# Two products of the same weights by one matmul of 512 columns in four residual stages

## The chip, the cores and the metric

The kernel runs on one core of a Trainium2 chip. The metric is the device time of one execution in microseconds (us), taken as the median of several. A profiled execution gives a trace; its span is the time from its first to its last instruction.

## The reference

Two blocks work on x of 256 tokens by 1024 features. Each adds to x what gated branches bring. Only the shape of the places where x is changed matters here:

```python
# first block, layer 0: z = h @ w_in, a convolution branch y_a and a recurrent branch y_b
return jnp.concatenate([y_a, y_b], axis=-1) @ p["w_out"], hT
# first block, layer 1: pooled branch
return (y * jax.nn.silu(g)) @ p["w_out"]
# both layers
x = x + gate[:, None] * out_x
# second block: token mixers end in a product with w_o, then the feed-forward part
x = x + mod[:, 2, None] * mix_x
x = x + mod[:, 5, None] * swiglu(h2, w_up[l], w_down[l])
```

After each of these four additions comes a norm over the 1024 features of x (the root of the mean of squares), and the next stage starts from the normed x. All inputs are fp32.

## The kernel before

**Layout.** Everything is feature-major: x is [128, 8, 256], eight slices of 128 features with all 256 tokens (`T`) as columns. A product with weights is made one output tile of 128 features at a time. A weight tile is [128, 8, 128], 512 KB, and SP loads them from one stream into a ring of six buffers `raw` (L420); a load waits until the tile six places ahead of it has been used. `ORDER` fixes the order of all tiles.

**Two halves.** fp32 precision is made from two fp32r halves. ScalarE rounds each weight tile to its high half `w_hi` (`highs`, L980). VectorE subtracts to get the low half `w_lo` (`lows`, L1415). Activations are split in the same way, for instance `ya_hi` and `ya_lo`. A product is then three matmuls for each of the eight slices k (`three`, L582 to L584): w_hi by hi, w_hi by lo, w_lo by hi, each 256 columns wide, all added up in the left half of one PSUM bank. `thirds` does this for one tile; `three` is also used with 512 columns in xb, where two token sets stand side by side in the bank. Four banks `ps` are used in turn. A bank's semaphore `ps_free` counts up when its reader is through with it.

**The four residual stages.** They are ya/yb (two weight tiles for each slice t of x), oa/ob (two), wo (one) and d0/d1/d2 (three, with 22 slices k in all). In ya/yb and oa/ob four tiles of the first kind come first, then the four of the second that add to the same banks, and then the same again. When a slice t is complete, VectorE's `add_to_x` (L1735) adds gate times bank to x[:, t]; its last line counts up the bank's semaphore. ScalarE waits for that and squares the slice (`squares`, L1216). In oa/ob it squares twice, once scaled (L1257). POOL adds up the first seven squares (L481), and TensorE sums over the features with `two_chunks` (L546, L548).

**What stands in a row around it.** The order on each engine is written by hand. In ya/yb, oa/ob and d, `add_to_x` first calls `ahead`, which makes the low halves up to four tiles ahead, and then does the x step; so on VectorE an x step stands behind a w_lo. In wo it is the other way: x step, `ahead` by two tiles, then `xb_lo` (L2157), which needs `xb_hi` of ScalarE (L1376). On ScalarE, `done` makes the high halves up to four tiles ahead, then waits for the tile, and the square follows. In the first half of ya/yb VectorE also does four `mod_tiles` steps (L1449), each of which waits for a DMA that POOL issues. After oa/ob TensorE does f 0, then `two_chunks` for the new squares, then f 1 to f 3. After ya/yb it only runs matmuls of ones (`keep_busy`) around `two_chunks`, until the normed slices h1 come.

Of the kernel before, what the change touches and what calls it, by code (L numbers as in the profile page):

```python
# [19 lines left out]
F32 = mybir.dt.float32  # L20
F32R = mybir.dt.float32r
I32 = mybir.dt.int32
ALU = mybir.AluOpType
# [4 lines left out]
T = 256  # L28
# [125 lines left out]
def build(nc, ins, out):  # L154
    with ExitStack() as ctx:
        base = nc.sbuf_base + (-nc.sbuf_base) % 32

        def at(name, kib, shape, dt=F32):
            return nc.alloc_sbuf_tensor_at(name, [P] + shape, dt, offset=base + int(kib * 1024))
# [47 lines left out]
        XW = T + SCONV_TAPS  # L207
        rs = at("rs", W + 106.25, [2, T])
        ga = at("ga", W, [KT, T])
        ya_hi = at("ya_hi", W, [KT, T], F32R)  # L210
        conv = at("conv", W + 8, [KT, T])
        UW = T + CONV_TAPS + 1
        RW = T + CONV_TAPS - 3
# [6 lines left out]
        yb_hi = at("yb_hi", W + 24, [KT, T], F32R)  # L220
        yb_lo = at("yb_lo", W + 40, [KT, T], F32R)
        ya_lo = at("ya_lo", W + 48, [KT, T], F32R)
        LB = 4
        PAIR_BUF = (0, 2, 0, 2)
        la = at("la", W + 48, [LB, 2, 2 * T])
# [15 lines left out]
        y_hi = at("y_hi", W + 78, [16, T], F32R)  # L241
# [3 lines left out]
        y_lo = at("y_lo", W + 97.25, [16, T], F32R)  # L245
        yt = at("yt", W + 16, [4, 2, T])


# [37 lines left out]
        m_hi, m_lo = at("m_hi", W + 60, [KT, T], F32R), at("m_lo", W + 88, [KT, T], F32R)  # L286
# [6 lines left out]
        ff_hi, ff_lo = at("ff_hi", W + 32, [FT, T], F32R), at("ff_lo", W + 54, [FT, T], F32R)  # L293
# [98 lines left out]
        def psum_of(name, t):  # L392

            return ps[PLACE[(name, t)][0]]
# [115 lines left out]
        def _(pe):  # L510
# [75 lines left out]
            def thirds(name, t, hi, lo, width=T, ready=None, tiles=KT, first=True, last=True):  # L586
# [7 lines left out]
                               last and k == tiles - 1)  # L594
                mm.then_inc(tile_done, 1)

            def side_by_side(tiles, hi, lo, ready, take=True, last=True):

                for k in range(KT):
                    pe.wait_ge(ready[0], ready[1] + k + 1)  # L600
                    for name, t in tiles:
                        wh, wl = split_weights(name, t)
                        o = bank_of(name, t) if k == 0 and take else psum_of(name, t)
                        mm = three(o[:, 0:T], wh[:, k, :], wl[:, k, :], hi(k), lo(k), k == 0, last and k == KT - 1)
                        if k == KT - 1:
                            mm.then_inc(tile_done, 1)
# [121 lines left out]
            ya = (lambda k: ya_hi[:, k, :], lambda k: ya_lo[:, k, :])  # L728
            yb = (lambda k: yb_hi[:, k, :], lambda k: yb_lo[:, k, :])
            for t in range(4):  # L730
                thirds("ya", t, *ya, last=False, ready=(ya_ready, 0) if t == 0 else None)
            for t in range(4):
                thirds("yb", t, *yb, first=False, ready=(yb_ready, 0) if t == 0 else None)
            for t in range(4, KT):
                thirds("ya", t, *ya, last=False)
            for t in range(4, KT):
                thirds("yb", t, *yb, first=False)


            keep_busy(4)  # L740
# [17 lines left out]
                mm.then_inc(tile_done, 1)  # L758
            for t0_ in range(0, KT, 4):
                for t in range(t0_, t0_ + 4):  # L760
                    thirds("oa", t, lambda k: y_hi[:, k, :], lambda k: y_lo[:, k, :], last=False,
                           ready=(y_ready, 0) if t == 0 else None)
                for t in range(t0_, t0_ + 4):
                    thirds("ob", t, lambda k: y_hi[:, KT + k, :], lambda k: y_lo[:, KT + k, :], first=False,
                           ready=(y_ready, KT) if t == 0 else None)


            both = ((h2o_hi, h2o_lo), (h2c_hi, h2c_lo))
# [162 lines left out]
            for t in range(HEADS):  # L931
                for name, hi, lo, ready in (("pa", oa_hi, oa_lo, oa_ready), ("pb", ob_hi, ob_lo, ob_ready)):
# [8 lines left out]
            wh, wl = split_weights("wo", 0)  # L941
            o = bank_of("wo", 0)
            for k in range(KT):
                pe.wait_ge(m_ready, k // 2 + 1)
                mm = three(o[:, 0:T], wh[:, k, :], wl[:, k, :], m_hi[:, k, :], m_lo[:, k, :], k == 0, k == KT - 1)
            mm.then_inc(tile_done, 1)
            for t in range(1, KT):
                thirds("wo", t, lambda k: m_hi[:, k, :], lambda k: m_lo[:, k, :])
            h3 = (lambda k: h3_hi[:, k, :], lambda k: h3_lo[:, k, :])
            xb = (lambda k: xb_hi[:, k, :], lambda k: xb_lo[:, k, :])  # L950
            for t in range(4):
# [6 lines left out]
                thirds("ub", t, *h3)  # L958
            for t in range(KT):
                for n, name in enumerate(("d0", "d1", "d2")):  # L960
                    thirds(name, t, lambda k: ff_hi[:, n * KT + k, :], lambda k: ff_lo[:, n * KT + k, :],
                           tiles=min(KT, FT - n * KT), first=(n == 0), last=(n == 2),
                           ready=(ff_ready, n * KT) if t == 0 else None)
            two_chunks(px[0], sq5, 8, 6 * KT)


# [438 lines left out]
        def _(v):  # L1405
# [723 lines left out]
            for t in range(HEADS):  # L2129
                e = t % 2  # L2130
                for part, (name, gate, gname) in enumerate((("pa", ga2, "ga2"), ("pb", gb2, "gb2"))):
                    done(name, t)
                    emptied(v, gname, 2 * t)
                    emptied(v, gname, 2 * t + 1)
                    if t >= 2:
                        v.wait_ge(m_ready, t - 1)
# [9 lines left out]
                v.tensor_tensor(m_lo[:, 2 * t:2 * t + 2, :], mt[:, e, 0], mh.bitcast(F32), ALU.subtract).then_inc(m_ready, 1)  # L2146
# [156 lines left out]
```

## Time and profile before

| | us |
|---|---|
| median of 3 runs | 906.0 |
| lowest, highest | 905.29, 907.52 |
| span of the profiled execution | 903.1 |

The engines in the profile are PE (TensorE's matmuls), PEld (its weight loads), DVE (VectorE), ACT (ScalarE), POOL and SP. Numbers with an L are lines of the kernel before. A matmul's recorded length contains its way through the array, so matmuls in a row overlap in the records; the distance from one start to the next is what counts. A step on DVE or ACT also overlaps the next one a little, if they don't depend on each other. In a timeline a row is one instruction or several of the same kind in a row, and in brackets stands how long the engine was idle before it and what ended that.

### The profile page before, as it was taken

To read this page: it belongs to the slowest core of one execution; us is meant where nothing else is said; L and a number is where in the kernel's file an instruction comes from. 1 tells how busy PE (TensorE), PEld (TensorE's weight loads), DVE (VectorE), ACT (ScalarE), POOL (GpSimd) and SP (SyncE) were. 2 spreads that over 40 slices of the span, in tenths; PEclk is the share of its full clock that TensorE was granted. 3 is DMA by queue.
4 is the path that set the end of the run, shared out by engine and by line. 5 is a ranking of instruction groups with operands and counts; after the bars stand their busy time and mean duration, and the time that the engine had idled before them with its cause. 6 is when DMAs were issued, how large, how long until landed. Compare 5 with 4: busy or idle time off the path is not lost.

```text
span 903.1 us, 17404 instructions
## 1 busy us (share of the span) xinstructions
PE 884.7 (98%) x7132; PEld 829.2 (92%) x7132; DVE 710.0 (79%) x1033; ACT 504.7 (56%) x727; POOL 142.2 (16%) x254
## 2 busy tenths in 40 slices
PE   8999999999999999999999999999999999999996
PEld 6688776689999999989999999999999999999995
DVE  5689667989888999968569975797987998765543
ACT  5474888997845455225554465483535644444441
POOL 0003864710021001300211100300001000000000
PEclk9999999999999999999999999999999999999998
DMA  9946987885776677866638844555556567666661
GB/s 365 388 144 216 306 271 222 280 274 181 214 276 210 230 262 269 293 215 201 184 103 292 303 128 142 178 173 187 155 180 181 172 204 255 187 185 183 196 204 52
DMA packets 55295, 195.45 MB, mean 216 GB/s; under 512 B 7856, under 2 KB 7984, under 8 KB 53808
## 3 DMA queue, kind: packets, MB, share of 16 engines
q1 hardware_dynamic: 39600, 147.73, 50.4%
q0 software_dynamic: 15616, 46.61, 15.2%
q8 instruction: 57, 0.93, 0.4%
q14 instruction: 22, 0.18, 0.1%
HBM read 188.60 MB, written 1.05 MB: 210 GB/s over the span
## 4 chain that ended last, share of the span: by engine, by line
PE 75%; DVE 14%; ACT 4%; issue 3%; DMA 2%; POOL 1%; DVEq 0%; SPq 0%; ACTq 0%; POOLq 0%
PE ps L582 22%; PE ps L584 21%; PE ps L583 21%; DVE w_lo L1415 4%; PE ps L756 3%; PE ps L685 2%; PE px L674 2%; ACT w_hi L980 1%; DVE win L1429 1%; DVE dump L1788 1%; DMA x<-in_xT 1%; DMA raw<-in_stream 1%; DVE li L1429 1%; PE px L861 1%; DVE li L1614 1%
## 5 line engine op out<-in xcount | busy, mean ns | idle before, releaser
L1415 DVE TENSOR_TENSOR w_lo<-raw,w_hi 128x1024 fp32r<-128x1024 f32 x232 | 280.5, 1226 | 83.9 <-ACT w_hi L980 83.3
L980 ACT ACTIVATE w_hi<-raw 128x1024 fp32r<-128x1024 f32 x232 | 242.7, 1055 | 110.8 <-DMA raw<-in_stream 110.0
L582 PE MATMUL ps<-h_hi,w_hi 128*128 128x256 f32 (+1 forms) x864 | 256.0, 296 | 6.2 <-DVE w_lo L1415 2.8
L583 PE MATMUL ps<-h_lo,w_hi 128*128 128x256 f32 (+1 forms) x864 | 251.4, 291 | 0.0
L584 PE MATMUL ps<-h_hi,w_lo 128*128 128x256 f32 (+1 forms) x864 | 251.3, 291 | 0.0
L582 PEld LDWEIGHTS ps<-h_hi,w_hi 128*128 128x128 f32 x864 | 165.3, 191 | 16.6 <-issue 5.7
L583 PEld LDWEIGHTS ps<-h_lo,w_hi 128*128 128x128 f32 x864 | 165.4, 191 | 3.5 <-issue 1.2
L584 PEld LDWEIGHTS ps<-h_hi,w_lo 128*128 128x128 f32 x864 | 165.4, 191 | 2.7
L459 POOL DMA_DIRECT2D modw<-in_mod_w x80 | 42.8, 536 | 391.6 <-DVE modw L1449 250.1
L582 PE MATMUL ps<-h2o_hi,w_hi 128*128 128x256 f32 x352 | 101.5, 288 | 0.0
L584 PE MATMUL ps<-h2o_hi,w_lo 128*128 128x256 f32 x352 | 99.6, 283 | 0.0
L583 PE MATMUL ps<-h2o_lo,w_hi 128*128 128x256 f32 x352 | 99.5, 283 | 0.0
L1449 DVE SCALAR_TENSOR_TENSOR modw<-modw,c_row 128x1024 f32<-128x1024 f32 x64 | 76.7, 1228 | 7.4 <-DMA modw<-in_mod_w 7.4
L582 PEld LDWEIGHTS ps<-h2o_hi,w_hi 128*128 128x128 f32 x352 | 67.4, 192 | 0.8 <-issue 0.2
L583 PEld LDWEIGHTS ps<-h2o_lo,w_hi 128*128 128x128 f32 x352 | 67.5, 192 | 0.3 <-issue 0.2
L584 PEld LDWEIGHTS ps<-h2o_hi,w_lo 128*128 128x128 f32 x352 | 67.4, 192 | 0.0
L468 POOL DMA_DIRECT2D shifts<-upad x128 | 62.7, 498 | 22.6 <-DVE upad L1572 16.8
L481 POOL TENSOR_TENSOR sq<-sq 128x256 f32<-128x256 f32 x24 | 18.6, 776 | 267.1 <-ACT sq L1219 267.1
L582 PE MATMUL ps<-ff_hi,w_hi 128*128 128x256 f32 x176 | 49.8, 283 | 0.0
L583 PE MATMUL ps<-ff_lo,w_hi 128*128 128x256 f32 x176 | 49.8, 283 | 0.0
L584 PE MATMUL ps<-ff_hi,w_lo 128*128 128x256 f32 x176 | 49.8, 283 | 0.0
L1219 ACT ACTIVATE sq<-x 128x256 f32<-128x256 f32 x32 | 13.2, 414 | 53.5 <-DVE x L1741 53.4
(353 smaller groups left out, 1856.6 us busy)
## 6 DMA issues: line engine op xcount, KB each, us to landing
raw<-in_stream SPq DMA_DIRECT2D x252, 512.0 KB, 3.8
modw<-in_mod_w POOLq DMA_DIRECT2D x80, 512.0 KB, 5.7
m<-in_mod_w SPq DMA_DIRECT2D x8, 1024.0 KB, 19.5
shifts<-upad POOLq DMA_DIRECT2D x128, 35.5 KB, 4.7
c_row<-in_c_rows SPq DMA_DIRECT2D x3, 512.0 KB, 7.6
ctxT<-in_ctxT SPq DMA_DIRECT2D x1, 1024.0 KB, 4.9
x<-in_xT SPq DMA_DIRECT2D x1, 1024.0 KB, 7.1
ctx2T<-in_ctx2T SPq DMA_DIRECT2D x1, 1024.0 KB, 6.5
```

The source lines that it names most:

```text
L459: pool.dma_start(modw[j][:], ins["mod_w"][t]).then_inc(modw_in[j], 16)
L468: pool.dma_start(shifts[t % 2][32 * d:32 * d + 32, g, :], upad[32 * g:32 * g + 32, t % 3, d:d + RW]).then_inc(shifts_in[t % 2], 16)
L481: a = pool.tensor_tensor(dst, src[:, 0, :] if k == 1 else dst, src[:, k, :], ALU.add)
L582: pe.matmul(o, wh, hi, start=start, stop=False)
L583: pe.matmul(o, wh, lo, start=False, stop=False)
L584: return pe.matmul(o, wl, hi, start=False, stop=stop)
L674: mm = pe.matmul(px[b][:, :], w[:, 4 * e + b, :], xpad[:, head, :, SCONV_LEFT:SCONV_LEFT + T], start=True, stop=True)
L685: mm = pe.matmul(o[c, 0:T], w[:, n, c], shifts[t % 2][:, g, 4 * n:4 * n + T], start=(n == 0), stop=(n == QUADS - 1))
L756: mm = pe.matmul(o[:, e * T:(e + 1) * T], w[:, 4 * e + k, :], d_in[:, 4 * (t // 2) + k, :], start=(k == 0), stop=(k == 3))
L980: act.activation(w_hi[split[0] % HI_RING][:], raw[n % RING][:], ACT.Copy).then_inc(w_hi_ready, 1)
L1415: v.tensor_tensor(w_lo[n % RING][:], raw[n % RING][:], w_hi[split[0] % HI_RING][:].bitcast(F32), ALU.subtract).then_inc(w_lo_ready, 1)
L1449: v.scalar_tensor_tensor(out=modw[s][:], in0=modw[s][:], scalar=1.0, in1=c_row[:, row, :], op0=ALU.mult, op1=ALU.mult, accum_out=mod[:, t: ...
```

## The change

A new helper `two_halves` takes both halves of the activations as one operand of 512 columns. w_hi times [hi, lo] fills both halves of the bank, w_lo times hi adds to the left half. For each k there are two matmuls where there were three. To make that one operand, hi and lo are allocated as one tensor (`ya_both` and so on); `y_lo` and `m_lo` move to other addresses by this, the others keep theirs. The last slice, t = 7, still goes by `thirds`. `add_to_x` has a second step for t < 7: it adds gate times the right half first, waits for its own write (`S.sync`), and then adds gate times the left half and frees the bank. `m_ready` counts slices instead of pairs of slices.

```diff
+            def two_halves(name, t, halves_of, ready=None, tiles=KT, first=True, last=True):
+
+                if t == KT - 1:
+                    thirds(name, t, lambda k: halves_of(k)[:, 0, :], lambda k: halves_of(k)[:, 1, :], ready=ready,
+                           tiles=tiles, first=first, last=last)
+                    return
+                wh, wl = split_weights(name, t)
+                o = bank_of(name, t) if first else psum_of(name, t)
+                for k in range(tiles):
+                    if ready is not None:
+                        pe.wait_ge(ready[0], ready[1] + k + 1)
+                    h = halves_of(k)
+                    pe.matmul(o[:, :], wh[:, k, :], h, start=first and k == 0, stop=False)
+                    mm = pe.matmul(o[:, 0:T], wl[:, k, :], h[:, 0, :], start=False, stop=last and k == tiles - 1)
+                mm.then_inc(tile_done, 1)
...
-                thirds("ya", t, *ya, last=False, ready=(ya_ready, 0) if t == 0 else None)
+                two_halves("ya", t, ya, last=False, ready=(ya_ready, 0) if t == 0 else None)
...
                 xt = x[:, t, :]
+                if t < KT - 1:
+                    S.do(v.scalar_tensor_tensor(out=xt, in0=psum_of(name, t)[:, T:2 * T], scalar=gate[:, t:t + 1],
+                                                in1=xt, op0=ALU.mult, op1=ALU.add))
+                    S.sync()
                 v.scalar_tensor_tensor(out=xt, in0=psum_of(name, t)[:, 0:T], scalar=gate[:, t:t + 1],
                                        in1=xt, op0=ALU.mult, op1=ALU.add).then_inc(free_of(name, t), 1)
```

TensorE at the start of ya, before (lines L582 to L584 are `three`; numbers behind the names are buffers):

```order
L582 MATMUL ps<-ya_hi,w_hi_65 128x256
L583 MATMUL ps<-ya_lo,w_hi_65 128x256
L584 MATMUL ps<-ya_hi,w_lo_59 128x256
L582 MATMUL ps<-ya_hi,w_hi_65 128x256
L583 MATMUL ps<-ya_lo,w_hi_65 128x256
```

and now (lines of the changed kernel):

```order
L611 MATMUL ps<-ya_both,w_hi_65 128x512
L612 MATMUL ps<-ya_both,w_lo_59 128x256
L611 MATMUL ps<-ya_both,w_hi_65 128x512
L612 MATMUL ps<-ya_both,w_lo_59 128x256
L611 MATMUL ps<-ya_both,w_hi_65 128x512
```

The first two matmuls of each k have become one. In all TensorE has 5473 rows where it had 5907.

VectorE in the second half of yb, from x step 4 to the rows after x step 7, before:

```order
L1741 SCALAR_TENSOR_TENSOR x<-ps,small,x 128x256
L1415 TENSOR_TENSOR w_lo_58<-raw_52,w_hi_64 128x1024
L1741 SCALAR_TENSOR_TENSOR x<-ps,small,x 128x256
L1415 TENSOR_TENSOR w_lo_59<-raw_53,w_hi_65 128x1024
L1741 SCALAR_TENSOR_TENSOR x<-ps,small,x 128x256 x2
L1415 TENSOR_TENSOR w_lo_60<-raw_54,w_hi_66 128x1024
```

and now:

```order
L1752 SCALAR_TENSOR_TENSOR x<-ps,small,x 128x256
L1755 SCALAR_TENSOR_TENSOR x<-ps,small,x 128x256
L1425 TENSOR_TENSOR w_lo_58<-raw_52,w_hi_64 128x1024
L1752 SCALAR_TENSOR_TENSOR x<-ps,small,x 128x256
L1755 SCALAR_TENSOR_TENSOR x<-ps,small,x 128x256
L1425 TENSOR_TENSOR w_lo_59<-raw_53,w_hi_65 128x1024
L1752 SCALAR_TENSOR_TENSOR x<-ps,small,x 128x256
L1755 SCALAR_TENSOR_TENSOR x<-ps,small,x 128x256 x2
L1425 TENSOR_TENSOR w_lo_60<-raw_54,w_hi_66 128x1024
```

Between two low halves of weights there are now two x steps. Nothing else on VectorE has moved, and ScalarE, POOL and SP have the same rows as before.

## Rows read from the trace of the kernel before

**Rows 1.** The page: span, and TensorE's share (busy us, share, instructions).

```profile
span 903.1 us, 17404 instructions
...
PE 884.7 (98%) x7132; PEld 829.2 (92%) x7132; DVE 710.0 (79%) x1033; ACT 504.7 (56%) x727; POOL 142.2 (16%) x254
```

**Rows 2.** Timeline of TensorE, 60 to 81 us: start, length, instruction, count.

```profile
60.21 0.39 PE L582 MATMUL ps<-h_hi,w_hi 128*128 128x512 f32 x1
...
74.94 0.39 PE L584 MATMUL ps<-h_hi,w_lo 128*128 128x512 f32 x1
75.17 0.28 PE L582 MATMUL ps<-h_hi,w_hi 128*128 128x256 f32 x1
...
75.40 0.28 PE L584 MATMUL ps<-h_hi,w_lo 128*128 128x256 f32 x1
...
80.80 0.28 PE L584 MATMUL ps<-h_hi,w_lo 128*128 128x256 f32 x1
```

**Rows 3.** Busy time by stretches: length, then each engine's busy us.

```profile
core 0: us, PE busy (x) PEld busy (x) DVE busy (x) ACT busy (x) POOL busy (x), PEclk, DMA share, GB/s
...
411.00:457.00 46.00, 46.00 (x385) 45.97 (x384) 31.59 (x52) 25.88 (x40) 7.38 (x11) 1.00 0.60 185
...
830.00:893.30 63.30, 63.30 (x530) 63.30 (x529) 29.63 (x32) 26.40 (x35) 4.44 (x6) 1.00 0.52 159
893.30:903.00 9.70, 1.27 (x6) 0.46 (x4) 4.67 (x5) 1.29 (x3) 0.00 (x0) 0.65 0.28 108
```

**Rows 4.** Timeline of VectorE in yb.

```profile
260.18 1.23 DVE L1449 SCALAR_TENSOR_TENSOR modw<-modw,c_row 128x1024 f32<-128x1024 f32 x1 [1.31 <-DMA modw<-in_mod_w]
...
276.91 0.48 DVE L1741 SCALAR_TENSOR_TENSOR x<-ps,small,x 128x256 f32<-128x256 f32 x1
...
280.02 0.48 DVE L1741 SCALAR_TENSOR_TENSOR x<-ps,small,x 128x256 f32<-128x256 f32 x1
281.50 0.48 DVE L1741 SCALAR_TENSOR_TENSOR x<-ps,small,x 128x256 f32<-128x256 f32 x1 [1.00 <-PE ps L584]
```

**Rows 5.** Timeline of ScalarE in yb.

```profile
271.56 1.06 ACT L980 ACTIVATE w_hi<-raw 128x1024 fp32r<-128x1024 f32 x1 [1.09 <-DMA raw<-in_stream]
...
280.60 0.42 ACT L1219 ACTIVATE sq<-x 128x256 f32<-128x256 f32 x1 [1.75 <-DVE x L1741]
280.92 1.04 ACT L980 ACTIVATE w_hi<-raw 128x1024 fp32r<-128x1024 f32 x1
282.08 0.42 ACT L1219 ACTIVATE sq<-x 128x256 f32<-128x256 f32 x1
```

**Rows 6.** Timeline of VectorE in ob.

```profile
429.83 0.48 DVE L1741 SCALAR_TENSOR_TENSOR x<-ps,small,x 128x256 f32<-128x256 f32 x1
...
440.38 0.48 DVE L1741 SCALAR_TENSOR_TENSOR x<-ps,small,x 128x256 f32<-128x256 f32 x1
...
447.57 1.23 DVE L1415 TENSOR_TENSOR w_lo<-raw,w_hi 128x1024 fp32r<-128x1024 f32 x1 [0.19 <-ACT w_hi L980]
...
459.26 0.48 DVE L1741 SCALAR_TENSOR_TENSOR x<-ps,small,x 128x256 f32<-128x256 f32 x1
```

**Rows 7.** Timeline of TensorE after f 0.

```profile
459.91 0.28 PE L584 MATMUL ps<-h2c_hi,w_lo 128*128 128x256 f32 x1
...
460.70 0.70 PE L548 MATMUL px<-sq,ones_p 128*128 128x256 f32 x2
```

**Rows 8.** Timeline of VectorE: two steps, the second needs the first.

```profile
461.44 0.42 DVE L1884 TENSOR_SCALAR vr<-px 128x256 f32<-128x256 f32 x1 [1.70 <-PE px L548]
461.90 0.29 DVE L1886 TENSOR_SCALAR vr<-vr 128x256 f32<-128x256 f32 x1
```

**Rows 9.** Timeline of VectorE in wo, two x steps in a row.

```profile
696.54 0.48 DVE L1741 SCALAR_TENSOR_TENSOR x<-ps,small,x 128x256 f32<-128x256 f32 x1 [0.38 <-PE ps L584]
...
699.42 0.48 DVE L1741 SCALAR_TENSOR_TENSOR x<-ps,small,x 128x256 f32<-128x256 f32 x1 [0.38 <-PE ps L584]
```

**Rows 10.** Timeline of VectorE: the last x step.

```profile
893.47 0.48 DVE L1741 SCALAR_TENSOR_TENSOR x<-ps,small,x 128x256 f32<-128x256 f32 x1 [7.43 <-PE ps L584]
```

More of the change, by code:

```diff
@@ L209, in build @@
         ga = at("ga", W, [KT, T])
-        ya_hi = at("ya_hi", W, [KT, T], F32R)
+        ya_both = at("ya_both", W, [2, 6, KT, T], F32R)[:, :, 0]
+        ya_hi, ya_lo = ya_both[:, 0], ya_both[:, 1]
         conv = at("conv", W + 8, [KT, T])
@@ L219, in build @@
         gb = at("gb", W + 16, [KT, T])
-        yb_hi = at("yb_hi", W + 24, [KT, T], F32R)
-        yb_lo = at("yb_lo", W + 40, [KT, T], F32R)
-        ya_lo = at("ya_lo", W + 48, [KT, T], F32R)
+        yb_both = at("yb_both", W + 24, [2, 2, KT, T], F32R)[:, :, 0]
+        yb_hi, yb_lo = yb_both[:, 0], yb_both[:, 1]
         LB = 4
@@ L240, in build @@
         win = [at("win0", W + 68, [16, PW]), at("win1", W + 73, [16, PW])]
-        y_hi = at("y_hi", W + 78, [16, T], F32R)
+        y_both = at("y_both", W + 78, [2, 16, T], F32R)
+        y_hi, y_lo = y_both[:, 0], y_both[:, 1]
         vr1 = at("vr1", W + 94, [T])
@@ L244, in build @@
         h1_lo = at("h1_lo", W + 105.25, [KT, T], F32R)
-        y_lo = at("y_lo", W + 97.25, [16, T], F32R)
         yt = at("yt", W + 16, [4, 2, T])
@@ L285, in build @@
         ob_hi, ob_lo = at("ob_hi", W + 24, [HEADS, T], F32R), at("ob_lo", W + 28, [HEADS, T], F32R)
-        m_hi, m_lo = at("m_hi", W + 60, [KT, T], F32R), at("m_lo", W + 88, [KT, T], F32R)
+        m_both = at("m_both", W + 60, [2, KT, T], F32R)
+        m_hi, m_lo = m_both[:, 0], m_both[:, 1]
         mt = at("mt", W + 96.25, [2, 2, 2, T])
@@ L292, in build @@
         h3_hi, h3_lo = at("h3_hi", W + 16, [KT, T], F32R), at("h3_lo", W + 24, [KT, T], F32R)
-        ff_hi, ff_lo = at("ff_hi", W + 32, [FT, T], F32R), at("ff_lo", W + 54, [FT, T], F32R)
+        ff_both = at("ff_both", W + 32, [2, FT, T], F32R)
+        ff_hi, ff_lo = ff_both[:, 0], ff_both[:, 1]
         v4 = at("v4", W + 76, [2, T])
@@ L727, in _ @@
                 thirds("gb", t, *own)
-            ya = (lambda k: ya_hi[:, k, :], lambda k: ya_lo[:, k, :])
-            yb = (lambda k: yb_hi[:, k, :], lambda k: yb_lo[:, k, :])
+            ya = lambda k: ya_both[:, :, k, :]
+            yb = lambda k: yb_both[:, :, k, :]
             for t in range(4):
-                thirds("ya", t, *ya, last=False, ready=(ya_ready, 0) if t == 0 else None)
+                two_halves("ya", t, ya, last=False, ready=(ya_ready, 0) if t == 0 else None)
             for t in range(4):
-                thirds("yb", t, *yb, first=False, ready=(yb_ready, 0) if t == 0 else None)
+                two_halves("yb", t, yb, first=False, ready=(yb_ready, 0) if t == 0 else None)
             for t in range(4, KT):
-                thirds("ya", t, *ya, last=False)
+                two_halves("ya", t, ya, last=False)
             for t in range(4, KT):
-                thirds("yb", t, *yb, first=False)
+                two_halves("yb", t, yb, first=False)
             keep_busy(4)
@@ L760, in _ @@
                 for t in range(t0_, t0_ + 4):
-                    thirds("oa", t, lambda k: y_hi[:, k, :], lambda k: y_lo[:, k, :], last=False,
-                           ready=(y_ready, 0) if t == 0 else None)
+                    two_halves("oa", t, lambda k: y_both[:, :, k, :], last=False, ready=(y_ready, 0) if t == 0 else None)
                 for t in range(t0_, t0_ + 4):
-                    thirds("ob", t, lambda k: y_hi[:, KT + k, :], lambda k: y_lo[:, KT + k, :], first=False,
-                           ready=(y_ready, KT) if t == 0 else None)
+                    two_halves("ob", t, lambda k: y_both[:, :, KT + k, :], first=False,
+                               ready=(y_ready, KT) if t == 0 else None)
             both = ((h2o_hi, h2o_lo), (h2c_hi, h2c_lo))
@@ L940, in _ @@
                     mm.then_inc(tile_done, 1)
[L941 to L948, printed above, removed]
+            for t in range(KT):
+                two_halves("wo", t, lambda k: m_both[:, :, k, :], ready=(m_ready, 0) if t == 0 else None)
             h3 = (lambda k: h3_hi[:, k, :], lambda k: h3_lo[:, k, :])
@@ L960, in _ @@
                 for n, name in enumerate(("d0", "d1", "d2")):
-                    thirds(name, t, lambda k: ff_hi[:, n * KT + k, :], lambda k: ff_lo[:, n * KT + k, :],
-                           tiles=min(KT, FT - n * KT), first=(n == 0), last=(n == 2),
-                           ready=(ff_ready, n * KT) if t == 0 else None)
+                    two_halves(name, t, lambda k: ff_both[:, :, n * KT + k, :], tiles=min(KT, FT - n * KT),
+                               first=(n == 0), last=(n == 2), ready=(ff_ready, n * KT) if t == 0 else None)
             two_chunks(px[0], sq5, 8, 6 * KT)
@@ L2135, in _ @@
                     if t >= 2:
-                        v.wait_ge(m_ready, t - 1)
+                        v.wait_ge(m_ready, 2 * t - 2)
                     v.tensor_tensor(mt[:, e, part], psum_of(name, t)[:].rearrange("p (n t) -> p n t", n=2),
```

2 lines of the change are left out of this document (1 added, 1 removed).

## The prediction, made before the changed kernel was run

> **What bounds the kernel now.** I read the page's busy times first: TensorE is busy 98% of a span of 903.1 us [rows 1]. The median of the runs is 906.0 us, 2.9 us more than the span of the profiled execution; I make the sum against 903.1 and add 2.9.
>
> A busy engine whose instructions overlap says little about a rate, so the second view is the timeline of TensorE where widths change [rows 2]. The 512-column matmuls of xb start from 60.21 to 74.94 us, 65 intervals, 0.2267 us apart. The 256-column ones start from 75.40 to 80.80 us, 45 intervals, 0.1200 us apart. Two of 256 take 0.2400 us where one of 512 takes 0.2267: a merged pair saves 0.0133 us. The columns are the same number, so what is saved is a fixed part of each matmul.
>
> Third, the table by stretches: in 411 to 457 us (oa, ob) and in 830 to 893.3 us (d0 to d2) TensorE works without a gap at full granted clock [rows 3], so a shorter stream would count there in full, unless something else ends later. So the fourth view is the timelines of VectorE and ScalarE at the ends of the four stages. There the two engines pass work back and forth in a ring: x += gate*bank (VectorE), square (ScalarE), the high half of a coming weight tile (ScalarE), its low half (VectorE), and the next x step, queued behind that low half. In yb one round takes 280.02 - 276.91 = 3.11 us [rows 4]. In ob, where ScalarE squares twice, it is (440.38 - 429.83)/3 = 3.52 us [rows 6]. A weight tile lasts 24 x 0.12 = 2.88 us on TensorE. The ring is already slower than TensorE in both stages; the weights made four tiles ahead hide it, and only the last square shows. In ob TensorE ends tile f 0 with 459.91, then waits for the squares: the second pair starts at 460.70 [rows 7].
>
> **What is removed.** In seven of eight column tiles of each stage, two matmuls become one: 7 x 16 = 112 pairs in ya/yb, 112 in oa/ob, 56 in wo, 7 x 22 = 154 in d, together 434, which is also what the order shows. At 0.0133 us that is 5.8 us of TensorE's time. The 512 to 256 change itself is in the trace: 74.94 to 75.17 [rows 2], no extra. Bounds for a pair: nothing saved (0), or both fixed parts gone (0.0267). I take 0.0133, a row of this kernel with the same operand form.
>
> The Trainium skill (TensorE: Matmul & The Clock Gate, section Back-to-back issue gap) gives an isolated matmul a fixed part of about 2.5 ns beside its columns. By that rule 434 pairs save 1.1 us instead of 5.8. The trace disagrees: 120.0 ns for 256 columns and 226.7 for 512 leave 13.3 ns [rows 2].
>
> **What is added.** Seven x steps per stage become two dependent ones. A step lasts 0.48 us [rows 4]. A dependent VectorE step starts 0.04 us after the end of the one before: 461.44 + 0.42 = 461.86, next at 461.90 [rows 8]. So the free signal that ScalarE's square waits for comes e = 0.52 us later (bounds: 0.40, if the steps overlapped as independent ones do, to 0.6). This is inside the ring. Spare time doesn't help: ScalarE's idle 1.75 us ends with x [rows 5].
>
> **ya/yb.** The first rounds hold mod steps. The second of those waits 1.31 us for a DMA [rows 4], which swallows the first two e: x 2 starts only 0.1 us later. Then x 3 is 0.5 later, x 4 0.6 (the wait of 1.09 us for the weights of ou 0 [rows 5] takes up the rest), x 5 1.1, x 6 1.65. The square of x 6 comes after its second step, 280.60 + 1.65 + 0.52 = 282.77. Behind it on ScalarE stands w_hi for ou 3 (0.32 us later, 1.04 us long), then the last square: 284.2 instead of 282.08 [rows 5]. Tile yb 7 itself is done at about the same time as before: TensorE saves 1.5 us here too, and I expect similar waits for the low halves of ya 7 and yb 4, which the ring delivers later. After the last square everything is a chain: statistics, root, h1, first matmul of ou. **+2.1 us.** Bounds: +1.0 (e at its low end, more taken up by the DMA waits) to +2.8.
>
> **oa/ob.** The x steps run from 429.83 to 459.26 without TensorE deciding any of them [rows 6]. Seven x steps come before the last one, and each gets e: 3.64, less the 0.19 us wait before w_lo at 447.57 [rows 6], which disappears: 3.4. The last x step starts at 462.7. In the middle the ring delivers weights too late for the faster stream. The low half of oa 7 ends where x 3 starts, 440.38 + 3e = 441.9; TensorE asks for it after eleven tiles of 2.773 us from 411.0, at 441.5, and waits some 0.5 us. The low half of ob 4 ends one round after x 3, 440.38 + 3.52 + 4e = 446.0, asked for at 441.9 + 2.8 = 444.7: 1.3 us. The two waits eat the 14 x 0.107 = 1.5 us that TensorE saves. TensorE then reaches the squares after f 0 at about the same time as now and finds them missing until 464.1 instead of 460.7 [rows 7]. The order of TensorE is fixed, so f 1 to f 3, which could fill the gap, are queued behind this wait. **+3.4 us**, bounds +2.3 to +4.2.
>
> **wo.** Here x comes before w_lo, and VectorE idles 0.38 of the 699.42 - 696.54 = 2.88 us per tile [rows 9], so it needs 2.50. With e it needs 3.02 against 2.77 of TensorE: VectorE becomes the limit from tile 3 on. The tiles' low halves come late from wo 6 on, and ua 0 starts about 0.3 us earlier than now; the low half of ub 0 then costs about 0.3. **0**, bounds -0.6 to +0.8. The first tile gains nothing, as it waits for m.
>
> **d.** One x step per three tiles, about every 8 us, so the ring has room. 154 x 0.0133 = **-2.05 us**, bounds 0 to -2.3. The last x step waits 7.43 us for TensorE [rows 10]; the last tile keeps its three matmuls and one step, and the tail stays. SP's and POOL's queues are not changed.
>
> **Sum.** 2.1 + 3.4 + 0 - 2.05 = +3.45 us: a span of 906.6, a time of **909.5 us**.
>
> **Rivals.**
> - The ring swallows e, since both of its engines stand idle in each round (ScalarE 1.75 us [rows 5]). Then TensorE's gain stays, less 0.25 us in wo 0: 906.0 - 5.5 = 900.5 us, faster. For it: that idle time. Against: it ends with VectorE's x step, which stands behind a low half that waits for ScalarE's high half: a closed ring. It decides where the last square comes later than 0.5 us before TensorE asks. Chance 0.11.
> - The ring costs e but more is absorbed, in DMA waits and in the overlap of the two steps: +1 and +2 us instead of 2.1 and 3.4, and wo gains 0.5. Sum 1 + 2 - 0.5 - 2 = +0.5: 906.5 us. Chance 0.27.
> - The merged matmul saves nothing when it alternates with a narrow one, or only the page's 2.5 ns. No row shows a steady alternation. The ring's costs stay, d gives 0: 911.5 us. By the page's rule d gives 0.4, and the time would be 911.1. Chance 0.11.
> - The wait of 3.4 us after f 0 lets TensorE's clock fall. In the trace it is 1.00 in both long stages and 0.65 in the last stretch, where TensorE is mostly idle [rows 3]. If it falls to the lower level (1.2 GHz) for some microseconds, +2 to +4 us more: 912.5. No row of the trace shows a wait of this length amid the kernel. Chance 0.08.
>
> **Numbers.** My forecast has 0.43, its own range 907.2 to 911.6. A measurement of this kernel can tell about 0.3% (2.7 us) from no change. Slower by more: most of my forecast (0.38), both last rivals (0.19), together 0.57. Within: the second rival and the low edge of the forecast, 0.32. Faster 0.11. Range 905.5 to 912.8: it leaves out the first rival and a part of the others.
>
> **What would show it.** Right: matmuls of 512 columns about 0.227 us apart from the following one and 0.120 before the next; the round in ob about 4.04 us and in yb about 3.63; the last ob square near 463.3 plus the shift from ya/yb (2.1); a TensorE wait of over 3 us after f 0, waiting on ScalarE's squares; short waits on w_lo in oa 7, ob 4, ya 7, yb 4; the d stage 2 us shorter. Wrong: rounds still at 3.1 and 3.5 us, or the two steps 0.40 us apart.

## The result and the profile after

| | before | changed |
|---|---|---|
| median of 6 runs each, us | 905.75 | 912.54 |
| lowest, highest | 905.29, 907.52 | 910.49, 918.95 |
| span of the profiled execution | 903.1 | 909.2 |

The changed kernel takes 1.0074 times as long, with an interval of 1.0051 to 1.0097. It is slower by 6.8 us, where 3.5 was forecast. (A ratio need not be that of the two medians.) The time is inside the range, but the sum is off by half of the result, and the rest of this text is mostly about where that half comes from.

The page of the changed kernel, span and TensorE's line, beside [rows 1]:

```profile
span 909.2 us, 16568 instructions
...
PE 883.3 (97%) x6698; PEld 806.1 (89%) x6698; DVE 722.2 (79%) x1061; ACT 503.7 (55%) x727; POOL 142.9 (16%) x254
```

TensorE has 434 matmuls less, and its busy time is 1.4 us shorter. VectorE has 28 steps more and is busy 12.2 us longer. Neither number tells the result. For that the places of the forecast have to be read one by one.

**The ring in yb.** The timeline of VectorE of the changed kernel (start, length, instruction, count, and in brackets the idle time before it and what ended that), to be laid beside [rows 4]:

```profile
276.26 0.47 DVE L1752 SCALAR_TENSOR_TENSOR x<-ps,small,x 128x256 f32<-128x256 f32 x1
276.77 0.48 DVE L1755 SCALAR_TENSOR_TENSOR x<-ps,small,x 128x256 f32<-128x256 f32 x1
278.75 1.23 DVE L1425 TENSOR_TENSOR w_lo<-raw,w_hi 128x1024 fp32r<-128x1024 f32 x1 [1.50 <-ACT w_hi L990]
279.89 0.48 DVE L1752 SCALAR_TENSOR_TENSOR x<-ps,small,x 128x256 f32<-128x256 f32 x1
```

The second step starts 0.51 us after the first (276.77), and the square on ScalarE waits for the second. The round is 279.89 - 276.26 = 3.63 us, before it was 3.11. VectorE's idle time before a low half is still 1.50 us, ended by ScalarE's high half, and on ScalarE the idle time before a square still ends with the x step. Nobody in this ring is busy all the time, and still each round costs the whole step more.

The timeline of ScalarE at the end of yb, to be laid beside [rows 5]:

```profile
284.61 0.42 ACT L1229 ACTIVATE sq<-x 128x256 f32<-128x256 f32 x1 [2.27 <-DVE x L1755]
284.94 1.04 ACT L990 ACTIVATE w_hi<-raw 128x1024 fp32r<-128x1024 f32 x1
285.88 0.40 ACT L1229 ACTIVATE sq<-x 128x256 f32<-128x256 f32 x1
```

The last square starts at 285.88. In this execution ya began 1.62 us later than in the profile before (a scatter of the part ahead of the change, see below), so it is 284.26 on the clock of the forecast, which had 284.2.

**The ring in ob**, VectorE again, beside [rows 6]:

```profile
433.86 0.48 DVE L1752 SCALAR_TENSOR_TENSOR x<-ps,small,x 128x256 f32<-128x256 f32 x1
...
437.89 0.48 DVE L1752 SCALAR_TENSOR_TENSOR x<-ps,small,x 128x256 f32<-128x256 f32 x1
...
466.64 0.48 DVE L1755 SCALAR_TENSOR_TENSOR x<-ps,small,x 128x256 f32<-128x256 f32 x1
```

The round is 4.03 us (before 3.52), and the last x step starts 32.78 us after the first, where before it was 29.43 us.

**TensorE in oa 7.** Two rows of two timelines, VectorE's and TensorE's:

```profile
444.82 1.23 DVE L1425 TENSOR_TENSOR w_lo<-raw,w_hi 128x1024 fp32r<-128x1024 f32 x1 [1.89 <-ACT w_hi L990]
...
447.11 0.36 PE L584 MATMUL ps<-y_both,w_hi 128*128 128x256 f32 x1 [0.78 <-DVE x L1755]
```

The low half of oa 7 is ready at 446.05, and TensorE's last matmul before the tile starts at 446.06. What it waits for is its bank: the second x step of slice 3, which frees it, starts at 446.48 and ends at 446.96. In ya 7 the same wait is 0.66 us.

**TensorE after f 0**, beside [rows 7]. The timeline, and then two stretches of the table by windows (length, and each engine's busy us and instructions, then the granted clock PEclk, the DMA share and GB/s):

```profile
464.35 0.28 PE L586 MATMUL ps<-h2c_hi,w_lo 128*128 128x256 f32 x1
465.67 0.70 PE L548 MATMUL px<-sq,ones_p 128*128 128x256 f32 x2 [1.04 <-POOL sqc L483]
468.08 0.70 PE L550 MATMUL px<-sq,ones_p 128*128 128x256 f32 x2 [1.71 <-ACT sqc L1267]
468.62 0.59 PE L548 MATMUL px<-sqc,ones_p 128*128 128x256 f32 x2
...
469.29 0.47 PE L584 MATMUL ps<-h2c_hi,w_hi 128*128 128x256 f32 x1
```

```profile
463.00:466.00 3.00, 1.96 (x16) 1.73 (x14) 1.07 (x3) 1.76 (x3) 1.42 (x2) 1.00 0.83 309
466.00:469.00 3.00, 1.29 (x6) 0.84 (x5) 1.30 (x3) 0.91 (x3) 0.00 (x0) 1.00 0.20 73
```

From the last matmul of f 0 to the first of f 1 it is 4.94 us where it was 2.0. TensorE waits for POOL's sum and for ScalarE's last square, and f 1 to f 3 stand behind the wait. The granted clock stays 1.00 here in this execution.

**The alternation in d**, TensorE, the view that no row of before could show:

```profile
859.77 0.40 PE L611 MATMUL ps<-ff_both,w_hi 128*128 128x512 f32 x1
860.01 0.28 PE L612 MATMUL ps<-ff_both,w_lo 128*128 128x256 f32 x1
860.13 0.40 PE L611 MATMUL ps<-ff_both,w_hi 128*128 128x512 f32 x1
860.37 0.28 PE L612 MATMUL ps<-ff_both,w_lo 128*128 128x256 f32 x1
```

Over the pairs of d, a wide matmul is followed after 0.236 us on average and a narrow one after 0.117. One slice k takes 0.3533 us. Three matmuls of 256 took 0.3600, and the forecast had 0.3467. The merged pair saves 6.7 ns and not 13.3. A wide one by turns takes 10 ns more than in a row of wide ones, and a narrow one 3 ns less than in a row of narrow ones.

**Stretch by stretch.** The part ahead of the four stages differs from one execution to the next, with any of the kernels: ya begins between 234.9 and 243.4 us in the profiles that follow. The largest part of this arises at 104 to 108 us, where TensorE waits for a low half. In the second profile of the kernel before that wait is 2.01 us, and on VectorE the low half stood behind a step that had waited 1.51 us for a transfer of modulation weights. Behind the wait the granted clock falls to 0.50 for 3.4 us. The same fall, of 3.4 or 6.8 us, is there in five of the thirteen profiles, with the kernel before among them, behind waits of 1.81 to 4.61 us. This scatter stands in every median. So I count from ya's first matmul, by the starts in TensorE's timelines (us):

| | ya to f 0 | f 0 to h2o | h2o to m | m to xb | xb to last sum | all |
|---|---|---|---|---|---|---|
| before | 221.93 | 13.58 | 207.43 | 23.94 | 191.17 | 658.05 |
| before, again | 221.82 | 13.59 | 207.47 | 24.66 | 191.18 | 658.72 |
| changed | 224.75 | 16.52 | 207.44 | 23.73 | 190.21 | 662.65 |
| changed, again | 224.79 | 18.13 | 207.43 | 23.64 | 190.20 | 664.19 |
| changed, third | 224.82 | 18.08 | 207.44 | 23.94 | 190.25 | 664.53 |
| changed, fourth | 225.19 | 16.52 | 207.44 | 23.84 | 190.23 | 663.22 |
| step alone | 224.22 | 17.70 | 207.42 | 23.94 | 191.14 | 664.42 |
| merge alone | 220.74 | 14.77 | 207.45 | 23.74 | 190.12 | 656.82 |
| before, x first | 221.83 | 13.24 | 207.42 | 24.11 | 191.15 | 657.75 |
| changed, x first | 221.13 | 13.24 | 207.43 | 23.86 | 190.21 | 655.87 |
| changed, by width | 224.67 | 18.18 | 207.42 | 24.47 | 189.61 | 664.35 |
| changed, both | 220.55 | 13.24 | 207.44 | 24.98 | 189.65 | 655.86 |
| changed, sums after f 1 | 224.78 | 13.63 | 207.93 | 23.87 | 190.25 | 660.46 |

"ya to f 0" holds ya/yb, what lies between, and oa/ob. "f 0 to h2o" is f 0 to f 3 with the sums of the squares. wo is "m to xb", and d is in the last column but one. The mean of the four profiles of the changed kernel is 663.6, that of the two of before 658.4: 5.3 us. The first two columns bring 6.7 us more, the fourth and fifth 1.5 less. The last rows of the table are the experiments.

### The profile page after: what moved, and what is told of

Its sections match the earlier page's. It is cut to its first block, busy times and chain, and to the rows that moved or that the text cites. A ratio compares the mean times of both kernels' runs of the same rounds, so it can differ in the third digit from the quotient of the medians.

```text
span 909.2 us, 16568 instructions
## 1 busy us (share of the span) xinstructions
PE 883.3 (97%) x6698; PEld 806.1 (89%) x6698; DVE 722.2 (79%) x1061; ACT 503.7 (55%) x727; POOL 142.9 (16%) x254
## 4 chain that ended last, share of the span: by engine, by line
PE 59%; DVE 23%; ACT 8%; issue 6%; DMA 3%; POOL 1%; DVEq 0%; SPq 0%; ACTq 0%
PE ps L584 14%; PE ps L586 14%; PE ps L585 14%; DVE w_lo L1425 9%; PE ps L611 5%; ACT w_hi L990 3%; PE ps L612 3%; PE px L692 2%; PE ps L774 2%; DVE stmp L1562 1%; DVE modw L1459 1%; PE ps L703 1%; DVE win L1439 1%; DVE dump L1802 1%; DMA raw<-in_stream 1%
## 5 line engine op out<-in xcount | busy, mean ns | idle before, releaser
L584 PE MATMUL ps<-h_hi,w_hi 128*128 128x256 f32 (+1 forms) x864 | 256.0, 296 | 8.0 <-DVE w_lo L1425 4.2
L584 PEld LDWEIGHTS ps<-h_hi,w_hi 128*128 128x128 f32 x864 | 165.3, 191 | 18.5 <-DVE w_lo L1425 6.7
L584 PE MATMUL ps<-h2o_hi,w_hi 128*128 128x256 f32 x352 | 101.5, 288 | 0.0
L584 PEld LDWEIGHTS ps<-h2o_hi,w_hi 128*128 128x128 f32 x352 | 67.5, 192 | 0.8 <-issue 0.2
L611 PE MATMUL ps<-ff_both,w_hi 128*128 128x512 f32 x154 | 54.5, 399 | 0.0
L612 PE MATMUL ps<-ff_both,w_lo 128*128 128x256 f32 x154 | 43.3, 281 | 0.0
L611 PE MATMUL ps<-y_both,w_hi 128*128 128x512 f32 x112 | 39.9, 401 | 0.0
```

The lines of the kernel that those rows point to most:

```text
L584: pe.matmul(o, wh, hi, start=start, stop=False)
L611: pe.matmul(o[:, :], wh[:, k, :], h, start=first and k == 0, stop=False)
L612: mm = pe.matmul(o[:, 0:T], wl[:, k, :], h[:, 0, :], start=False, stop=last and k == tiles - 1)
```

## The experiments

The theory: the second x step costs e = 0.5 us in every round of a ring of VectorE and ScalarE, and the merged matmul gives back part of it, in d alone. The rivals: the merged matmul itself brings the loss (other waits, other banks), or the ring is not closed and something else paces it, or the loss is scatter.

### Both kernels once more

No edit: the same two kernels, timed and profiled again.

> The kernel before, once more, with a profile. Question: in the trace of the changed kernel the last x step of ob came 7.4 us later than before, but 1.6 us of it was there at 188 us, ahead of any changed instruction. If that is chance (theory 1), the stretch up to 188 us varies by 1 to 2 us from one execution of this same kernel to the next, and the time is within 0.3% of the kernel before. If the change causes it (theory 2), the gate product of 188.5 us (VectorE, L1597) starts within 0.3 us of 188.5 here.

Measured: the kernel before again is 908.77 us. All the runs of the kernel before in the same session have a median of 906.41, and the ratio to them is 1.0011 (0.9978 to 1.0044). The gate product that was to tell the two theories apart starts at 193.9 us, where it started at 188.5. Nothing was changed, so a shift of this size ahead of ya is chance.

> The changed kernel once more, with a profile. Both theories: about +6.5 us (912.3). Chance: the product that started at 190.1 us in its first trace moves by 1 us or more in either direction, and the last x step of d moves with it. Cause: it stays at 190.1 within 0.3 us. In both, the stage lengths stay: from the first x step of yb to the last square 28.98 us, from the first x step of ob to the last 32.78 us, within 0.1.

Measured: 911.99 us, a ratio of 1.0064 (1.0036 to 1.0092). The gate product moved too, from 190.1 to 196.1 us, and the stage lengths stayed (29.00 and 32.78 us). The loss is no scatter. But the second profile has what the first didn't. The stretch from f 0 to h2o takes 1.61 us longer than in the first, and the windows of TensorE there are, for the changed kernel again:

```profile
470.00:472.00 2.00, 0.96 (x7) 0.75 (x6) 0.48 (x1) 1.49 (x3) 1.42 (x2) 1.00 0.93 355
472.00:474.00 2.00, 0.39 (x2) 0.00 (x0) 1.14 (x2) 0.76 (x3) 0.00 (x0) 1.00 0.22 77
474.00:476.00 2.00, 1.89 (x5) 1.56 (x6) 0.72 (x2) 0.23 (x3) 0.00 (x0) 0.59 0.00 0
476.00:478.00 2.00, 2.00 (x10) 1.82 (x10) 0.60 (x2) 0.76 (x2) 0.00 (x0) 0.55 0.00 0
478.00:480.00 2.00, 2.00 (x20) 2.00 (x19) 1.97 (x2) 0.00 (x0) 0.00 (x0) 1.00 0.03 8
```

and three rows of its timeline:

```profile
476.81 0.41 PE L585 MATMUL ps<-h2c_lo,w_hi 128*128 128x256 f32 x1
477.03 0.41 PE L586 MATMUL ps<-h2c_hi,w_lo 128*128 128x256 f32 x1
477.24 0.41 PE L584 MATMUL ps<-h2c_hi,w_hi 128*128 128x256 f32 x1
```

After 4 us in which TensorE worked 1.35 us, the granted clock falls to the lower level (1.2 GHz). The two means of 0.59 and 0.55 make (0.41 + 0.45) x 2 x 2 = 3.4 us at that level, in which half, 1.7 us, is lost. A 256-column matmul then follows the one before by 0.21 us instead of 0.12. That is the rival of the falling clock, and the first profile alone would have ruled it out.

### The step alone, and the merged matmul alone

The step alone: the kernel before, with a second x step that adds 0.0 times the same half of the bank. What is computed stays the same.

```diff
                 xt = x[:, t, :]
+                if t < KT - 1:
+                    S.do(v.scalar_tensor_tensor(out=xt, in0=psum_of(name, t)[:, 0:T], scalar=0.0,
+                                                in1=xt, op0=ALU.mult, op1=ALU.add))
+                    S.sync()
```

> The kernel before with three matmuls as it was, and only the second, dependent x step added in seven of eight slices of each stage (it adds 0.0 times the bank, so x is unchanged). Ring theory: ya/yb +2.1 us, oa/ob +3.4, wo +0.5 (VectorE needs 3.02 us where a tile takes 2.88), d 0: together +6.0 us, so about 911.8. Rounds of 3.63 us in yb and 4.03 in ob. Rival, the ring has room for the step and the loss comes from the merged matmuls: +1 us at most, rounds of 3.1 and 3.5.

Measured: 913.31 us, 1.0076 (1.0047 to 1.0104). The step alone brings the whole loss. From ya to h2o it takes 241.92 us, and the changed kernel takes 241.27 to 242.92. Its VectorE in ob:

```profile
433.87 0.42 DVE L1742 SCALAR_TENSOR_TENSOR x<-ps,x 128x256 f32<-128x256 f32 x1
434.32 0.48 DVE L1745 SCALAR_TENSOR_TENSOR x<-ps,small,x 128x256 f32<-128x256 f32 x1
...
437.84 0.42 DVE L1742 SCALAR_TENSOR_TENSOR x<-ps,x 128x256 f32<-128x256 f32 x1
```

This step is a little shorter, as its factor is a constant: the real step comes 0.45 us later instead of 0.51. The round is 3.97 us: 3.52 + 0.45. With e = 0.45 the way from x 0 to x 7 in ob is 2.92 us longer than before (6.5 e), with 0.51 it is 3.35 (6.6 e). The loss goes by e. wo and d don't change at all, so there the second step is free; the 0.5 us that was expected in wo isn't there. The clock falls in this profile too (17.70).

The merged matmul alone: the changed kernel without the second step. The right half of the bank, the product of w_hi and the low half of the activations, is left out of x.

```diff
                 xt = x[:, t, :]
-                if t < KT - 1:
-                    S.do(v.scalar_tensor_tensor(out=xt, in0=psum_of(name, t)[:, T:2 * T], scalar=gate[:, t:t + 1],
-                                                in1=xt, op0=ALU.mult, op1=ALU.add))
-                    S.sync()
```

> The changed kernel without the second x step: the right half of the bank is left out of x, so the low halves' share is missing from the result. It has all of the merged matmuls' gain and none of the step's cost. A merged pair saves 6.7 ns by the trace of the changed kernel. Ring theory: in ya/yb and oa/ob the ends are set by the rings, so nothing is gained there (0 to -0.3 each), wo -0.3, d -1.0: about -1.5 us, 904.3. Rival, TensorE sets the pace everywhere: 434 x 6.7 ns = -2.9 us, 902.9. By my prediction's 13.3 ns a pair it would have been -5.8.

Measured: 906.22 us, 0.9995 (0.9967 to 1.0023). The rounds stay at 3.51 us:

```profile
444.33 0.48 DVE L1751 SCALAR_TENSOR_TENSOR x<-ps,small,x 128x256 f32<-128x256 f32 x1
...
447.84 0.48 DVE L1751 SCALAR_TENSOR_TENSOR x<-ps,small,x 128x256 f32<-128x256 f32 x1
```

The table by stretches is the better witness. The merged matmul brings TensorE to f 0 1.19 us earlier (220.74 against 221.93), and between f 0 and h2o it gives back exactly 1.19 (14.77 against 13.58), since the squares come when the ring brings them. Of the 1.19 us, 0.45 come from ya/yb and 0.76 from oa/ob. The x steps of slices 0 to 3 of ob come no earlier after the start of oa than in the kernel before, so in oa/ob the gain turns into waiting. Those of slices 4 to 7 come 0.43 us later, since ScalarE in this execution waited 1.34 us for a weight of f 0. What is left is wo and d, 1.2 us. So in oa/ob a faster TensorE earned nothing, and in ya/yb at most 0.45 us.

### The ring opened: x step ahead of the last low halves

In the rounds the x step stands behind the low half of the tile four places ahead. Here only the tiles up to two ahead are made before the x step, as in wo, and the rest after it. With one step (on the kernel before) and with two (on the changed kernel):

```diff
-                    ahead(name, t)
+                    ahead(name, t, 2)
...
+                if name != "wo" and (t < KT - 1 or name == "ob"):
+                    ahead(name, t)
```

> The changed kernel, but in yb, ob and d the x steps come ahead of the low half of the tile four places on (before an x step only low halves up to two tiles on are made). This opens the ring: no x step waits for a high half that is made after the last square. Ring theory: in ya/yb and oa/ob TensorE sets the ends again. Against the kernel before: ya/yb -0.75 us (112 pairs at 6.7 ns), oa/ob -0.75 and -0.5 for the wait after f 0 that goes, wo and d -1.3 as in the changed kernel: -3.3 us, and TensorE's wait before the squares after f 0 under 0.3 us. Rival, VectorE's work as such is too much (the second steps, wherever they stand): +2 us or more against before.

> The kernel before with the same reordering of VectorE and nothing else. Ring theory: its ring cost it only the wait after f 0, so about -0.5 us against before; the last x step of ob then starts right after its tile, about 2 us earlier than now. Rival, the ring already cost the kernel before much: -2 us or more.

Measured: changed, x first: 905.38 us, 0.9965 (0.9931 to 0.9999). Before, x first: 905.49 us, 0.9976 (0.9944 to 1.0007). By the stretches the same edit is worth 7.8 us on the changed kernel (663.6 to 655.9) and 0.6 on the kernel before (658.4 to 657.8). About 0.8 of the 7.8 is the falling clock, which two of the four profiles of the changed kernel have. VectorE of the changed kernel with x first, in ob:

```profile
455.55 0.47 DVE L1752 SCALAR_TENSOR_TENSOR x<-ps,small,x 128x256 f32<-128x256 f32 x1
...
457.59 0.48 DVE L1752 SCALAR_TENSOR_TENSOR x<-ps,small,x 128x256 f32<-128x256 f32 x1
...
458.50 1.55 DVE L1425 TENSOR_TENSOR w_lo<-raw,w_hi 128x1024 fp32r<-128x1024 f32 x1
460.33 0.48 DVE L1755 SCALAR_TENSOR_TENSOR x<-ps,small,x 128x256 f32<-128x256 f32 x1 [0.28 <-PE ps L586]
```

Two steps and a low half now take 457.59 - 455.55 = 2.04 us, with no idle time between them, and the last x step waits for TensorE and not for the ring. The steps are as many and as long as in the changed kernel. Only the order is another, so the loss was the ring and not VectorE's work. In ya/yb it is gone as well: from ya to the first matmul behind the sums it takes 52.39 us, where the changed kernel takes 54.85 and the kernel before 52.46. TensorE then goes from the last matmul of f 0 to the sums without a wait: 13.24 us from f 0 to h2o.

The expectation for the changed kernel with x first was 3.3 us under the kernel before. The ratio makes 3.2 of it (0.1 to 6.3), the stretches 2.5, the medians 1.1: the forecast of this run holds, roughly. Against the kernel before, ya/yb gave nothing, where 0.75 us was expected. There TensorE still waited 0.5 us for a low half, and VectorE has the `mod_tiles` steps beside the x steps. One round of such a stretch, from the kernel of the next section but with the same order:

```profile
257.65 0.48 DVE L1754 SCALAR_TENSOR_TENSOR x<-ps,small,x 128x256 f32<-128x256 f32 x1
...
258.56 1.22 DVE L1427 TENSOR_TENSOR w_lo<-raw,w_hi 128x1024 fp32r<-128x1024 f32 x1
259.70 1.76 DVE L1461 SCALAR_TENSOR_TENSOR modw<-modw,c_row 128x1024 f32<-128x1024 f32 x1
...
261.39 0.47 DVE L1754 SCALAR_TENSOR_TENSOR x<-ps,small,x 128x256 f32<-128x256 f32 x1
```

3.74 us without a gap, for one tile's low half. TensorE uses one up in 2.8 us. So VectorE limits this stretch in this order too; the changed kernel's round there is 3.73 us. Of the 3.74 us, 1.69 are the `mod_tiles` step. It is recorded with 1.76 us here and with 1.22 in the changed kernel, which has 0.35 us of idle time before its low half instead. Why it is longer no run shows, and no order with the mod steps elsewhere was tried.

### The matmuls of a tile by width

To see what alternation costs, the changed kernel runs all wide matmuls of a tile and then all narrow ones:

```diff
                     pe.matmul(o[:, :], wh[:, k, :], h, start=first and k == 0, stop=False)
-                    mm = pe.matmul(o[:, 0:T], wl[:, k, :], h[:, 0, :], start=False, stop=last and k == tiles - 1)
+                for k in range(tiles):
+                    mm = pe.matmul(o[:, 0:T], wl[:, k, :], halves_of(k)[:, 0, :], start=False,
+                                   stop=last and k == tiles - 1)
```

> The changed kernel, with the wide matmuls of a tile in a row and its narrow ones behind them, in place of wide, narrow, wide, narrow. If the alternation is what costs 6.7 ns of the 13.3 that a merged pair should save, d gets 1.0 us shorter than in the changed kernel (52.9 + 136.8 us from the last wo x step to the last d x step become 188.7), while ya/yb and oa/ob, ends set by the ring, stay at 28.98 and 32.78. If a merged pair saves 6.7 ns whatever its neighbours are, nothing changes.

Measured: 913.75 us, 1.0051 (1.0021 to 1.008). The total can't show 1 us, the stretch can: xb to the last sum is 189.61 instead of 190.20 to 190.25 and 191.17. From the first matmul of d to the last sum it is 61.73 us, alternating it was 62.33, and before 63.36. The 154 pairs of d save 1.63 us against the kernel before, 10.6 ns each, where alternating they save 1.03, 6.7 ns each. The rows of TensorE:

```profile
863.19 2.00 PE L611 MATMUL ps<-ff_both,w_hi 128*128 128x512 f32 x8
865.03 1.11 PE L613 MATMUL ps<-ff_both,w_lo 128*128 128x256 f32 x8
```

The eight wide ones take 1.84 us, 0.230 each. Expected was 1.0 us more than alternating, and it gave 0.6: the direction is shown, the full 13.3 ns aren't reached even so. The rest of what it gives in d may be lost in wo. There the first tile runs while its activations come slice by slice. All wide matmuls first want them sooner: TensorE's wait for m is 1.6 us here and 2.2 in the next kernel, against 0.7 to 1.0 in the alternating ones. But the kernel before showed 0.6 once and 1.4 once without any change, so this is argued and not shown.

Both together, x first and by width:

> Both: the x steps ahead of the far low halves, and wide matmuls in a row. With 13.3 ns a pair in all stages and no ring: ya/yb -1.5 us, oa/ob -1.5 and -0.5, d -2.05, wo -0.3: -5.8 us against before, about 900.6. If grouping brings nothing: as after_xfirst, -3.3.

Measured: 903.27 us, 0.9962 (0.993 to 0.9995). It is the lowest median of all and faster than the kernel before, by 3.4 us of the ratio (0.5 to 6.3) and 2.5 us by the stretches, where it is level with "changed, x first" (655.86 and 655.87). Expected were 5.8. TensorE reaches f 0 1.3 us earlier than before and d is 1.6 us shorter, but m to xb is 24.98. The interval ends near 1, and whether it beats "changed, x first" can't be told.

### The sums after f 1

The wait after f 0 costs time only because f 1 to f 3 are queued behind it. One edit in TensorE's order of the changed kernel:

```diff
-                if t == 0:
+                if t == 1:
                     two_chunks(px[0], sq2, 4, 4 * KT)
                     two_chunks(px[2], sqc, 4, 4 * KT)
```

> The changed kernel with one edit in TensorE's order: the four matmuls that sum the squares stand after tile f 1 instead of after f 0. Theory (the 3.4 us of late squares count only because f 1 is queued behind them, and in some executions they also let the granted clock fall to 0.5 for about 2.5 us): f 1 fills the wait; the squares come at 468.1 us of the changed kernel's clock, f 1 ends at 467.3, so a wait of about 0.8 us is left; h2o 0 is asked for 3.1 us earlier, at 13.4 us after the start of f 0 instead of 16.5 to 18.2, and since its later slices come one per 0.79 us from 473.65 on, TensorE waits there some 1.2 to 1.5 us in all. Net 1.6 to 1.9 us less than the changed kernel without the fall of the clock, about 3.3 less than with it: 908.5 to 910.5 us beside 912. The granted clock stays 1.00 in this place. Rival (the norm after the squares decides, not the queue): the wait moves to h2o 0 in full, and the time is the changed kernel's.

Measured: 908.9 us, 1.0026 (1.0 to 1.0052). By the stretches that is 3.2 us under the mean of the changed kernel (660.46 against 663.65) and 2.2 under its fastest profile, which has no fall of the clock; by the medians 3.1 (against 911.99, taken in another session). TensorE there:

```profile
473.92 0.60 PE L548 MATMUL px<-sq,ones_p 128*128 128x256 f32 x2
474.64 0.70 PE L550 MATMUL px<-sq,ones_p 128*128 128x256 f32 x2
475.18 0.59 PE L548 MATMUL px<-sqc,ones_p 128*128 128x256 f32 x2
...
475.85 0.47 PE L584 MATMUL ps<-h2c_hi,w_hi 128*128 128x256 f32 x1
```

f 0 to h2o takes 13.63 us, as before the change, with the clock at 1.00. The norm behind the squares isn't the limit: expected were 1.2 to 1.5 us of waits for the slices of h2o, and all that shows is that the next stretch is 0.5 us longer. The squares are as late as in the changed kernel. So of the loss in these two columns about half (2.9 us without the fall of the clock, 4.5 with it) was the place of the wait in TensorE's order.

### How often the clock falls

Two more profiles of the changed kernel, without an edit.

> The changed kernel once more, for one more profile. The wait after f 0 is the same 3.2 to 3.5 us of which TensorE fills 1.2 with the sums. Theory (the granted clock falls behind this wait in most executions but not in all, and that is 1.6 us from one execution of the same program to another): from f 0 to h2o 0 either 16.5 us at clock 1.00 or about 18.1 with a fall to 0.5. Rival (the first profile is the odd one for another reason): other lengths.

> The same as the run before, for the share of executions with the fall: 16.5 us from f 0 to h2o 0, or about 18.1. With two of two at 18.1, four of five profiles with this wait have the fall, and the median of the changed kernel contains it.

Measured: 18.08 us from f 0 to h2o in the third, with windows at 0.59 and 0.56, and 16.52 in the fourth, with 1.00 all through. The waits are the same in both to 0.01 us, 1.03 and 1.71. Of the four profiles of the changed kernel two have the fall. The kernel with the matmuls by width (18.18) and the step alone (17.70) have it too. In the profiles without this wait the clock stays 1.00 at this place, and so it does in the merged matmul alone, with one wait of 1.26 us. Ahead of ya it falls behind other waits, in the kernel before too, as said above. So the wait makes the fall possible, and something that differs between executions of one program decides. The Trainium skill (TensorE: Matmul & The Clock Gate, Part 1: The HAM clock gate) says that the watch over TensorE's activity runs free and isn't reset when a kernel starts. That would fit two outcomes of one program, but no run here shows it.

## Why the forecast was right, and where it was off

- **The ring, right.** e was 0.52 and measured 0.51. The rounds were to be 3.63 and 4.04 and are 3.63 and 4.03. The idle times of both engines inside the ring did not take anything of e. The rival that they would is refuted by the step alone.
- **ya/yb and oa/ob, right within 0.3 us.** Forecast +2.1 and +3.4. From ya to the first matmul behind its sums the changed kernel takes 54.85 us in its first profile, before 52.46: +2.4. From oa to h2o it is 63.22 and 59.85: +3.4. Together +5.8. What the merged matmul gained was eaten on the way, but by another wait than forecast. The prediction had low halves that come late (0.5 us in oa 7, 1.3 in ob 4). TensorE waits for the bank that the second x step frees, 0.66 us in ya 7 and 0.78 in oa 7, while the low half is there, and in ob 4 there is a delay of 0.2 us only. The pairs gained half as much as was thought, 0.76 instead of 1.5 us in oa/ob, and the waits cost less too. TensorE reached the end of f 0 0.4 us later, and this had no effect, as the squares came later still. That the sums agree is in part luck.
- **wo, right within its scatter.** 0 forecast. m to xb is 23.64 to 23.94 against 23.94 and 24.66. VectorE did become the slower one, without idle time, while a tile takes 2.83 us on TensorE. Its cycle there is 2.93 us (698.24 to 701.16) and not 3.02, since the steps behind the x steps overlap a little:

```profile
698.24 0.47 DVE L1752 SCALAR_TENSOR_TENSOR x<-ps,small,x 128x256 f32<-128x256 f32 x1
...
701.16 0.47 DVE L1752 SCALAR_TENSOR_TENSOR x<-ps,small,x 128x256 f32<-128x256 f32 x1
```

- **d, the first term that was mis-sized.** Forecast -2.05, measured -1.03. The 13.3 ns came from 65 wide matmuls in a row and 45 narrow ones in a row [rows 2], while the changed kernel alternates them. I had seen one change of width at 74.94 us and taken it as "no extra", which is one interval of a view with two decimals. Alternating pairs save 6.7 ns. By width they save 10.6. The Trainium skill (TensorE: Matmul & The Clock Gate, section Back-to-back issue gap) had 2.5 ns of fixed part for a matmul by itself. The measured saving lies between that and [rows 2], and neither was right for this mix.
- **The clock, the second.** Forecast as a rival with a chance of 0.08 and +2 to +4 us. It happened in two of four profiles of the changed kernel, where it costs 1.6 us, and in both variants that kept the full wait. In the time of the median it adds something up to that. The argument against it was that no row showed such a wait. That was no argument.
- **The sum.** Forecast 2.1 + 3.4 + 0 - 2.05 = +3.45. The stretches give 5.8 - 0.2 - 1.0 = +4.6 without the fall, +6.2 with it. The two comparisons of medians gave 6.8 and 5.6. The first profile's span, 6.1 us longer, is right by chance: 1.6 of it is a late start of ya, ahead of everything that was changed.
- **The signs.** The rival of a merged matmul that saves nothing gave 911.5 and is wrong in its mechanism: it saves, in wo and d, by half of what was forecast.

## What to carry to other kernels

When two engines hand work back and forth in a fixed order, write down the round. A step added inside it costs its full length in every round, though both engines stand idle part of the time, and where the ring sets the end a faster third engine earns nothing. Here an order in which the step no longer stands behind the other engine's next delivery gave all of it back. And look at what is queued behind the wait that the ring ends in: here one line in TensorE's order, moving the sums of the squares behind one more tile of independent work, gave back 3 us. A rate taken from matmuls of one width in a row does not hold for a mix of widths.

## What was not expected of the hardware

- Wide and narrow matmuls by turns: 0.236 us behind a wide one and 0.117 behind a narrow one, against 0.2267 and 0.1200 in rows of one width. By turns they cost 6.6 ns per pair more than apart.
- A wait of 4 us in which TensorE works 1.35 us lets the granted clock fall to the lower level for about 3.4 us in some executions of a program and not in others, and costs 1.6 us. Ahead of ya it falls in five of thirteen profiles, the unchanged kernel's among them.
- With nothing changed in it, the part of the kernel ahead of ya takes 234.9 to 243.4 us. That is more than the whole effect that was to be measured, and why the stretches say more here than spans do.
